# Modulation in four feed-forward stages: chunk sums on four column quarters and transposes instead of single-column matmuls

## The reference, cut to what matters

```python
for l in range(DEPTH):
    mod = (jax.nn.silu(c) @ ada_w[l] + ada_b[l]).reshape(Bn, N_SUB, 3, D_MODEL)
    shift, scale, gate = mod[:, :, 0, None], mod[:, :, 1, None], mod[:, :, 2, None]
    h = x * (1.0 + scale[:, 0]) + shift[:, 0]
    y = swiglu(h, ffn_w1[l, 0], ffn_w3[l, 0], ffn_w2[l, 0])
    x = post_norm_residual(x, y, gate[:, 0], 0.5, ln_g[l, 0], ln_b[l, 0])
    ...
def swiglu(h, w1, w3, w2):
    return (jax.nn.silu(h @ w1) * (h @ w3)) @ w2
```

## Time and profile before

| | us |
|---|---|
| median of 3 runs (3762.21 to 3770.17) | 3767.84 |
| profiled run | 3761.1 |
| its span | 3759.3 |
| TensorE busy | 3588.2 |
| VectorE busy | 1981.8 |
| ScalarE busy | 1221.3 |

### The profile page before, as it was taken

One profiled execution on the slowest core, in us unless ns is written; L12 is line 12 of the kernel. 1 busy time (PEld: TensorE's weight loads), 2 busy tenths in 40 slices (PEclk: granted clock), 3 DMA queues, 4 the chain that ended last, 5 costly groups with the idle time before them and its releaser, 6 DMA issues. The chain is left out here.

```text
span 3759.3 us, 43412 instructions
## 1 busy us (share of the span) xinstructions
PE 3588.2 (95%) x17810; PEld 2961.3 (79%) x17810; DVE 1981.8 (53%) x3051; ACT 1221.3 (32%) x1916; POOL 149.1 (4%) x212
## 2 busy tenths in 40 slices
PE   6999999999999999999999998998999999989999
PEld 4888778678887888777678886787788878877887
DVE  5655566665456645566664355665322366553233
ACT  2223324532233222333532223634222354442222
POOL 1110100001000100100000001000000000000000
PEclk8999999999999999999999999999999999999999
DMA  6664321145443644321143331211233222113332
GB/s 238 227 198 135 78 86 46 51 143 187 140 140 102 222 159 135 96 68 46 51 129 116 111 132 46 79 34 51 79 101 123 96 48 72 40 51 98 93 107 79
DMA packets 438042, 397.75 MB, mean 106 GB/s; under 512 B 53779, under 2 KB 390275, under 8 KB 437844
## 3 DMA queue, kind: packets, MB, share of 16 engines
q1 hardware_dynamic: 413028, 310.53, 27.0%
q0 software_dynamic: 24816, 84.45, 6.6%
HBM read 390.14 MB, written 4.78 MB: 105 GB/s over the span
## 5 line engine op out<-in xcount | busy, mean ns | idle before, releaser
L163 PE MATMUL m_ps<-m_h_high,ffn_w_high 128*128 128x512 f32 x2100 | 823.8, 392 | 0.0
L164 PE MATMUL m_ps<-m_h_low,ffn_w_high 128*128 128x512 f32 x2100 | 819.3, 390 | 0.0
L165 PE MATMUL m_ps<-m_h_high,ffn_w_low 128*128 128x512 f32 x2100 | 819.2, 390 | 0.0
L165 PEld LDWEIGHTS m_ps<-m_h_high,ffn_w_low 128*128 128x128 f32 x2100 | 395.5, 188 | 83.4
L163 PEld LDWEIGHTS m_ps<-m_h_high,ffn_w_high 128*128 128x128 f32 x2100 | 396.2, 189 | 82.4
L164 PEld LDWEIGHTS m_ps<-m_h_low,ffn_w_high 128*128 128x128 f32 x2100 | 396.0, 189 | 81.6
L953 ACT ACTIVATE ffn_sil<-m_ps 128x512 f32<-128x512 f32 x132 | 79.1, 599 | 1139.0 <-PE m_ps L165 1139.0
L163 PE MATMUL m_ps<-ffn_w_high,ffn_hid_high 128*128 128x512 f32 x1056 | 412.3, 390 | 0.0
L165 PE MATMUL m_ps<-ffn_w_high,ffn_hid_low 128*128 128x512 f32 x1056 | 411.7, 390 | 0.0
L164 PE MATMUL m_ps<-ffn_w_low,ffn_hid_high 128*128 128x512 f32 x1056 | 411.4, 390 | 0.0
L993 DVE TENSOR_TENSOR ffn_hid<-ffn_sil,m_ps 128x512 f32<-128x512 f32 x110 | 75.6, 687 | 560.4 <-ACT ffn_sil L953 560.4
(11 more groups left out here) (470 smaller groups left out, 5564.1 us busy)
## 6 DMA issues: line engine op xcount, KB each, us to landing
m_raw<-in_ffn_w SPq DMA_DIRECT2D x176, 512.0 KB, 4.7
ffn_rows<-in_ada_w POOLq DMA_DIRECT2D x128, 512.0 KB, 5.0
ffn_rows<-in_ffn_w SPq DMA_DIRECT2D x88, 512.0 KB, 3.4
m_raw<-in_w_in SPq DMA_DIRECT2D x32, 1024.0 KB, 5.5
m_raw<-in_ffn_w_gate SPq DMA_DIRECT2D x44, 512.0 KB, 3.7
m_raw<-in_ffn_w_up SPq DMA_DIRECT2D x44, 512.0 KB, 4.8
ffn_rows<-in_ffn_w_down SPq DMA_DIRECT2D x44, 512.0 KB, 3.2
m_raw<-in_w_out SPq DMA_DIRECT2D x24, 512.0 KB, 4.4
```

The lines of the kernel that those rows point to most:

```text
L163: pe.matmul(out, sh, mh, start=first, stop=False, skip_group_check=True)
L164: pe.matmul(out, sh, ml, start=False, stop=False, skip_group_check=True)
L165: return pe.matmul(out, sl, mh, start=False, stop=last, skip_group_check=True)
```

## The change

The chunks are taken in groups of four (`ADA_SIDE`), so 3, 2, 3 and 1 groups in the four stages; the last group of the third stage and the only one of the fourth have two chunks.

- `sums_pe` replaces `columns_pe`'s old body: for each chunk of the group one matmul with 32 columns of ones as the stationary operand and the chunk's 512 columns as the moving one. Chunk t of the group goes to partitions 32 t to 32 t + 31 of bank 7, so to column quarter t of the array. It stands at the head of TensorE's pass F + 2, where F now belongs to the group's last chunk.
- `sums_dve` copies these rows out of PSUM into `ada_sums`, at the end of VectorE's pass F + 3, behind its pieces.
- `columns_pe` turns them with four transposes into bank 6, at the head of TensorE's pass F + 3. It waits for that copy.
- `columns_dve` places each chunk's four columns in `ada_cols`, at the end of VectorE's pass F + 4. `finish_dve` reads them from there.
- There are six parts instead of three, five of them in the last tiles of `hid`. So the wait for the tape's store moves from VectorE's pass 14 (before `hidden(12)`) to its pass 2.
- The pieces go into ada_last = FT - 8 = 14 passes instead of 15. In the first stage passes 2 to 15 get 3, 3, 4, 3, 4, 3, 4, 3, 3, 4, 3, 4, 3, 4 pieces; in the third 2, 3, 3, 3, 3, 3, 3, 2, 3, 3, 3, 3, 3, 3 (before, passes 2 to 16: 2, 3, 3, 2, 3, 3, 2, 3, 3, 2, 3, 3, 2, 3, 3).

By this dealing TensorE's transposes stand in passes 8, 13 and 17 of the first stage, 10 and 17 of the second, 9, 15 and 17 of the third, and 17 of the fourth. VectorE has no pieces left in pass 17.

```diff
-ADA_K, ADA_PARTS = 2, 3
+ADA_K, ADA_PARTS, ADA_SIDE = 2, 6, 4
...
         if k == 0 and chunk >= ADA_PARTS:
-            dve.wait_ge(S.ada_column, chunk - ADA_PARTS + 1)
+            dve.wait_ge(S.ada_column, (chunk - ADA_PARTS) // ADA_SIDE + 1)
...
-    def columns_pe(self, pe, S, chunk):
-
-        l, c = self.columns[chunk]
-        pe.wait_ge(S.ada_mac, DT * (chunk + 1))
+    def group(self, g):
+        return range(ADA_SIDE * g, min(ADA_SIDE * (g + 1), len(self.columns)))
+
+    def sums_pe(self, pe, S, g):
+
+        pe.wait_ge(S.ada_mac, DT * (self.group(g)[-1] + 1))
+        if g:
+            pe.wait_ge(S.ada_copied, g)
+        for t, chunk in enumerate(self.group(g)):
+            mm = pe.matmul(self.M.ps[32 * t:32 * (t + 1), 7, :], self.M.ones[:, 0:32], self.parts[chunk % ADA_PARTS], start=True, stop=True)
+        mm.then_inc(S.ada_column, 1)
+
+    def sums_dve(self, dve, S, g):
+
+        n = 32 * len(self.group(g))
+        dve.wait_ge(S.ada_column, g + 1)
+        if g:
+            dve.wait_ge(S.ada_turned, g)
+        dve.tensor_copy(self.sums[0:n, :], self.M.ps[0:n, 7, :]).then_inc(S.ada_copied, 1)
+
+    def columns_pe(self, pe, S, g):
+
+        n = 32 * len(self.group(g))
+        pe.wait_ge(S.ada_copied, g + 1)
+        if g:
+            pe.wait_ge(S.ada_placed, self.group(g)[0])
         for q in range(T // P):
-            mm = pe.matmul(self.M.ps[:, 7, 4 * c + q:4 * c + q + 1], self.part[:, chunk % ADA_PARTS, q * P:(q + 1) * P],
-                           self.M.ones[:, 0:1], start=True, stop=True)
-        mm.then_inc(S.ada_column, 1)
+            mm = pe.transpose(self.M.ps[:, 6, q * P:q * P + n], self.sums[0:n, q * P:(q + 1) * P], self.M.ident[0:n, 0:n])
+        mm.then_inc(S.ada_turned, 1)
+
+    def columns_dve(self, dve, S, g):
+
+        dve.wait_ge(S.ada_turned, g + 1)
+        turned = self.M.ps[:, 6, :].rearrange("p (q n) -> p q n", n=P)
+        for t, chunk in enumerate(self.group(g)):
+            c = self.columns[chunk][1]
+            dve.tensor_copy(self.cols[:, 4 * c:4 * (c + 1)], turned[:, :, 32 * t]).then_inc(S.ada_placed, 1)
...
-            ada.part = sb("ada_part", ADA_PARTS, T)
+            ada.parts = [hid[:, FT - 1 - n, :] for n in range(5)] + [sb("ada_part", T)[:]]
+            ada.sums, ada.cols = sb("ada_sums", T), sb("ada_cols", 72)
...
-        ada_last = FT - 7
+        ada_last = FT - 8
...
-                if ada and 1 <= f - 2 <= ada_last:
-                    for c in ada_chunks(f - 2):
-                        ada.columns_pe(pe, S, c)
+                for g in ada_groups(f - 2):
+                    ada.sums_pe(pe, S, g)
+                for g in ada_groups(f - 3):
+                    ada.columns_pe(pe, S, g)
...
+                if kept and f == 2:
+                    dve.wait_ge(M.tape_stored, 16)
                 ada_pieces(f - 1)
+                for g in ada_groups(f - 3):
+                    ada.sums_dve(dve, S, g)
+                for g in ada_groups(f - 4):
+                    ada.columns_dve(dve, S, g)
```

More of the change, by code:

```diff
@@ L349, in _ @@
             low(DT - 1)
-ADA_SIGNALS = " ada0_landed ada1_landed ada_mac ada_partial ada_column mod_chain mod_ready mod_turned mod_copied mod_stored"
-ADA_K, ADA_PARTS = 2, 3
+ADA_SIGNALS = " ada0_landed ada1_landed ada_mac ada_column ada_copied ada_turned ada_placed mod_chain mod_ready mod_turned mod_copied mod_stored"
+ADA_K, ADA_PARTS, ADA_SIDE = 2, 6, 4
 class Ada:
@@ L371, in sum @@
         chunk, k = n // (DT // ADA_K), ADA_K * (n % (DT // ADA_K))
-        part = self.part[:, chunk % ADA_PARTS, :]
+        part = self.parts[chunk % ADA_PARTS]
         dve.wait_ge([S.ada0_landed, S.ada1_landed][n % 2], 16 * (n // 2 + 1))
         if k == 0 and chunk >= ADA_PARTS:
-            dve.wait_ge(S.ada_column, chunk - ADA_PARTS + 1)
+            dve.wait_ge(S.ada_column, (chunk - ADA_PARTS) // ADA_SIDE + 1)
         for j in range(ADA_K):
@@ L404, in finish_dve @@
         link = chain(dve, S.mod_chain)
-        dve.wait_ge(S.ada_column, len(self.columns))
+        dve.wait_ge(S.ada_placed, len(self.columns))
         for part, l, s, at in self.places()[0]:
-            shift, scale, gate = (M.ps[:, 7, 24 * s + 8 * w:24 * s + 8 * (w + 1)] for w in range(3))
+            shift, scale, gate = (self.cols[:, 24 * s + 8 * w:24 * s + 8 * (w + 1)] for w in range(3))
             bias = [M.columns[:, l, 24 * s + 8 * w:24 * s + 8 * (w + 1)] for w in range(3)]
@@ L892, in _ @@
                     ada.load(pool, S, n)
-        ada_last = FT - 7
+        ada_last = FT - 8
         ada_at = [f * ada.pieces // ada_last for f in range(ada_last + 1)] if ada else None
-        ada_chunks = lambda f: [c for c in range(len(ada.columns)) if ada_at[f - 1] < 4 * (c + 1) <= ada_at[f]]
+        ada_groups = lambda f: [g for g in range(-(-len(ada.columns) // ADA_SIDE))
+                                if 1 <= f <= ada_last and ada_at[f - 1] < 4 * (ada.group(g)[-1] + 1) <= ada_at[f]] if ada else []
         @block.tensor
@@ L924, in _ @@
                 mm.then_inc(S.projected, 1)
-                if ada and f == ada_last + 3:
+                if ada and f == ada_last + 5:
                     ada.turn_pe(pe, S)
@@ L989, in hidden @@
             def hidden(f):
-                if kept and f == KEPT:
-                    dve.wait_ge(M.tape_stored, 16)
                 dve.wait_ge(S.silu_done, f + 1)
@@ L1019, in _ @@
                 split(f)
+                if kept and f == 2:
+                    dve.wait_ge(M.tape_stored, 16)
                 ada_pieces(f - 1)
+                for g in ada_groups(f - 3):
+                    ada.sums_dve(dve, S, g)
+                for g in ada_groups(f - 4):
+                    ada.columns_dve(dve, S, g)
                 if res and 2 <= f < 2 + TT:
                     res.tile_dve(dve, S, f - 2)
-                if ada and f == ada_last + 3:
+                if ada and f == ada_last + 4:
                     ada.finish_dve(dve, S)
-                if ada and f == ada_last + 5:
+                if ada and f == ada_last + 6:
                     ada.copy_dve(dve, S)
```

## The result

| | before | after |
|---|---|---|
| median, us (six runs each, side by side) | 3766.56 (3761.88 to 3770.17) | 3783.06 (3779.51 to 3788.42) |
| profiled run, us | 3761.1 | 3780.53 |
| its span, us | 3759.3 | 3778.7 |

The account below looks back on a forecast made before the run. TensorE, busy 95% of the span, was taken to bound the kernel. Stage losses of 12.3 and 12.4 less a gain of 3.9 made 20.8, plus 8 for the clock 28.8, onto the median 3767.84: 3796.6 us, range 3776 to 3812.

Parts of the forecast that it names:

- The wait for the end of the pass: TensorE's transposes wait for the copy at the end of VectorE's pass; first stage loses 12.3 us before the clock's cost.
- The third stage: Copies end at 1299.1 and 1372.6, pass 17's products start at 1397.1, before 1384.70; loss 12.4 us before the clock's cost.
- The price of four transposes: TensorE's turns: a set of four 128x128 transposes a group, 0.89 us each set.
- The price of the sums: TensorE's sums on array quarters, running side by side: 0.86 us and 0.09 for the edges, 0.95 a group.
- (c): Rival: copies land in time, TensorE's balance of 13.8 us is gained, 3754.0; chance 0.09.
- The clock: Half clock behind the four stops in stages one and three, 2.0 us each, 8 more in all.
- The tape: Wait for the tape's store, moved from pass 14 to pass 2, costed at nothing.
- (a): Rival: the stops come but the clock stays up, 3788.6; chance 0.20.
- (b): Rival: the sums' quarters run in a row, 9 us more, 3806; chance 0.12.
- the balance: Pure TensorE balance: 30.4 us of columns removed less nine groups of sums and turns, 13.8 gained.
- (d): Rival: the stops are half made good, each stage loses 5 instead of 12, about 3774; chance 0.09.

Follow-up runs that it names:

- e10: Changed kernel with three load slots and the copy ahead of the pieces, 14 passes: 3742.54 us against 3764.41 for the kernel before, ratio 0.9942.
- e13: The changed kernel run and profiled once more, unchanged: 3785.36 us against 3764.27 for the kernel before, ratio 1.0050.
- e8: The kernel before with three load slots for the pieces in place of two, nothing else: 3764.34 us against 3764.41, ratio 0.9999.
- e1: Changed kernel with VectorE's copy of the sums moved ahead of the pieces, 14 passes: 3760.93 us against 3765.01 for the kernel before, ratio 0.9989.
- e9: Changed kernel with 40, 22 and 16 useless products filling three of TensorE's four stops: 3775.41 us against 3762.70 for the kernel before, ratio 1.0036.
- e7: Changed kernel with the sums made on the whole array, only each group's last chunk kept: 3791.14 us against 3762.70 for the kernel before, ratio 1.0078.
- e5: Changed kernel with three load slots in place of two, copy behind the pieces, 14 passes: 3746.52 us against 3762.70 for the kernel before, ratio 0.9955.
- e3: Changed kernel with the copy ahead of the pieces and 15 passes: 3756.98 us, ratio 0.9985 to the kernel before.

## Why the prediction was right, and where it was not

It held in its direction and its range (3776 to 3812), and missed in size: 28.8 forecast, 16.5 and 21.1 measured at the medians, 24.5 and 25.5 in the four stages, of which alone its sum speaks.

- **The wait for the end of the pass.** Right, and in its sum almost to the tenth. Group 0's copy in the first stage was forecast for 162.9, and ends at 163.25. The products of pass 17 were forecast for 276 and start at 275.95. In part that is luck: up to that copy the four passes with three pieces took 12.1 us on average for 11.8, the three with four pieces 12.8 for 13.16, and the two errors cancel. The stage's loss is 15.8 for 16.3 (12.3 and twice 2.0), the second's gain 4.2 for 3.9, the fourth's nothing.
- **The third stage: 12.9 for 16.4 (12.4 and twice 2.0).** The stage began 10.3 late, and less that, its copies end at 1299.4 and 1371.2, forecast for 1299.1 and 1372.6: so the sum of the passes held (1.4 too long in the second). Here too errors cancelled: pass 4 took 16.05 for 14.26, with a wait of 5.37 for a load, and passes 6 to 8 took 34.4 for 36.0. The step that failed is the clock behind the first stop. I had costed a fall there; TensorE stood only 1.25 us and kept 1.00. It came late to this stop since it had already stood 2.23 and 3.14 us in the stage (1257.44, 1271.71), before its passes 5 and 6, waiting for splits behind passes of VectorE with three pieces and a residual tile. I had worked out those passes (14.3 us, VectorE's passes 4 and 5) for VectorE alone and never put TensorE's beside them. It changes nothing at the end, because VectorE's chain sets that, but it moves the stop, and with it 2.0 of the clock. The two misses, 2.0 and 1.4, make the 3.5.
- **The price of four transposes: mis-sized, 0.89 for 0.44.** I took the eight records of L587 for four transposes with two records each, as the f32 matmuls have. The row at 938.49 has four records for four transposes: one each, and the third product behind starts at 939.38, 0.44 later than without. L587 x8 are eight transposes.
- **The price of the sums: mis-sized the other way, 0.95 for 1.2.** The busy time is 1.06, but the third product behind 140.06 starts at 141.63; less two products of 0.227 and with 0.08 of gap ahead of it, that is 1.2. The change of form costs more on the path than its busy time says. Together a full group costs 1.65, not 1.84, and a pair, by the same counting, 1.8. This explains nearly all of what the change can gain: 12 x 0.95 - 3 x 1.65 = 6.4 in the first stage (e10: 6.3), 8 x 0.95 - 2 x 1.65 = 4.3 in the second (4.2), 9.5 - 3.3 - 1.8 = 4.4 in the third (4.3). Rival (c)'s 13.8 came near (15.3 by these prices, 14.8 in e10) because the two errors cancel in part.
- **The clock.** Three falls of 2.2 to 2.4 us behind the copy's stops, where I had four of 2.0. A further one, behind the wait for the split at 1271.71, costs TensorE's pass 2.7 us and the stage nothing.
- **The tape.** The wait for its store, now in pass 2, cost nothing, as assumed: VectorE goes from the split (77.32 to 79.61) straight to its first piece (79.53).
- **Beside the stages.** Between 24.5 and 16.5 lie 8.0 us. 2.9 are a matter of which run was profiled: 5.5 us below its median before, 2.5 after. The other 5.1 lie outside the four stages. In part the clock explains it: at the head of the third stage it returns 1.2 us sooner (below). For the rest I have only that the parts between the stages differ between two runs of the same kernel by 5 us (e13), and that e8, whose stages agree with before to 0.1, has a span 3.2 longer. In nearly every kernel of the table the medians come out below the sum of the stages, by up to 11 us (e1). Why, stays open.

The rivals: (a) fell with the clock of 0.50 behind three stops and with e9, though by size its 3788.6 was the nearest to 3783.06. That is luck: in the stages its 20.8 and the forecast's 28.8 lie about as far from 24.5. (b) fell with e7. (c), copies in time, did not come, but e5 comes near its condition (loads that land sooner), and in e10 every copy is in time and TensorE gains what the balance promised. (d), about 3774 for half the loss, is 9 us off, and the first stage's losses were not made good: 15.8 of 16.3.

## What to carry to other kernels

Before a wait is put at the head of the bound engine's queue, ask when the *last* instruction ahead of its releaser ends, and not whether the other engine has time in the mean: an engine at 53% was 11 us late. An engine's idle time that costs nothing today (67 us of waits for loads) is the first thing to look at when something new is hung behind it; here one moved line was worth about 20 us, and a third buffer more. Small steps that another engine waits for go ahead of the bulk work of a pass.

## What the runs showed of the hardware

The clock fell after shorter stops than I had looked for, and not by their length alone. In the kernel after it fell behind 3.14 us of idle time (1271.71, a product of 0.77) and stayed up behind 2.23; in e9 it fell behind 2.73 and stayed up behind 2.65. Other runs have the order turned round. Four transposes behind a stop, e3 in the first stage, e7 in the third:

```profile
212.65 1.12 PE L411 MATMUL m_ps<-m_ident,ffn_ada_sums 128*128 128x128 f32 x4 [2.19 <-DVE ffn_ada_sums L402]
...
1388.70 0.66 PE L411 MATMUL m_ps<-m_ident,ffn_ada_sums 128*128 128x128 f32 x4 [2.95 <-DVE ffn_ada_sums L402]
```

Behind 2.19 us the four run at the half clock (1.12), behind 2.95 at the full one (0.66). So the length of a stop doesn't say by itself what comes behind it; what else decides, no run here shows. The clock also returned at different times for the same code. Windows over the head of the third stage, from the first product behind the transposes, before and then after:

```profile
1187.53:1191.00 3.47, 3.47 (x8) 2.81 (x9) 3.06 (x8) 3.47 (x9) 1.41 (x2) 0.50 0.73 215
1191.00:1194.00 3.00, 3.00 (x10) 2.32 (x9) 2.52 (x3) 2.31 (x2) 0.00 (x0) 0.61 0.97 268
```

```profile
1199.07:1202.54 3.47, 3.47 (x9) 2.75 (x10) 3.06 (x8) 3.47 (x9) 1.41 (x2) 0.54 0.75 228
1202.54:1205.54 3.00, 3.00 (x15) 2.49 (x14) 2.51 (x3) 2.33 (x2) 0.00 (x0) 1.00 0.93 251
```

The same matmuls, behind nearly the same idle time (3.04 and 2.85 us ahead of the transposes before them): 36 records take 10.98 us before and 9.74 after, 1.2 us that no edit accounts for. An f32 matmul of 512 columns leaves two records, which start 0.43 us apart (e7: eight in 3.59), an f32 transpose of 128 columns one (938.49: four in 0.60). A set of sums on quarters costs 1.2 us of TensorE's path and one on the whole array 3.44 (e7).
